# Hybrid layer with a 32-expert mixture: the second norm in halves, the router's steps reordered, the last adaLN product moved, the first projection and the final norm split

## The chip, the cores and the metric

The kernel runs on one core of one Trainium2 chip. The metric is the device time of one execution in microseconds (us); the numbers below come from one execution taken by the hardware profiler and from three timed runs.

## The reference, cut to what matters

One layer on 256 rows of 1024 (two tiles of 128 rows). `w_ada` gives six rows of 1024 (shift, scale and gate of both norms), in 12 column blocks of 512.

```python
mod = silu(c) @ w_ada + b_ada;  sh1, sc1, gt1, sh2, sc2, gt2 = split(mod, 6)
h = rms_norm(x, g_norm1) * (1 + sc1) + sh1
z = h @ w_in + b_in                      # 5376 columns: v, u, q, k, v, gate A, gate B
...                                      # gated MLP (A) and window attention (B)
x = x + gt1 * ((sigmoid(ga) * (ya @ w_o_a) + sigmoid(gb) * (yb @ w_o_b)) @ w_out)
h2 = rms_norm(x, g_norm2) * (1 + sc2) + sh2
top_v, top_e = top_k(h2 @ w_router + b_router, 4)      # of 32 experts; gates = softmax(top_v)
# expert e on its rows: gu = h2 @ w_gate_up[e] + b_gate_up[e]   (1024 x 2048, f32, 8 MiB)
#   hid = min(gu[:, :1024], 7) * sigmoid(1.702 * ...) * (clip(gu[:, 1024:], -7, 7) + 1)
#   y = hid @ w_down[e] + b_down[e]                             (1024 x 1024, f32, 4 MiB)
x = x + gt2 * sum(gate * y);  return rms_norm(x, g_final)
```

## The kernel before, in words

Five instruction streams are written out by hand and tied by semaphores (`ev(name)`): `sp` (SyncE) issues the large loads in a fixed order, `pe` multiplies, `dve` and `act` do the elementwise work, `pool` a few constants. Each engine runs its own stream strictly in the written order, so a wait holds everything behind it on that engine.

**Dense part.** Each projection is cut into items of 512 columns, in the order v0, v1, u0, u1, q0, q1, kv, ga0, ga1, gb0, gb1, oa0, oa1, ob0, ob1, out0, out1. An item's weights (2 MiB) go to one of three ring slots. VectorE splits them into an upper part (`w_parts_upper`, L810) and a remainder (`lower`, L367), as it does with the activations (`x_parts`, L834). TensorE then runs `rows_times` for each row tile: 24 matmuls (L1363), eight each of upper by upper, lower by upper and upper by lower. The adaLN blocks are spread between the items: `ada(j)` (L1385), a ScalarE copy (`part_copy`), `late_rows(j)` (L1396) and VectorE's `add_mod(j)`. `ada(11)` makes the second half of `gt2`; it stands between gb0 and gb1, and its weights sit in the room of slots 6 and 7.

**Slots.** An expert's weights are 12 pieces of 1 MiB: eight of gate_up, four of down. 22 slots (`store`) hold them, in rooms that the dense part frees bit by bit, so `sp` fills the slots for the first 22 pieces (`first_loads`, L392 and L410) one after another: 0, 1, 5, 10 and 11 when out1 is done, 18 when h2 is there, 16 after `logit_parts`, 21 after the logits, 20 when `start_acc` has put x into the accumulators (`acc_set`), 14 and 15 after the table of blocks. From then on `refill` loads a piece as soon as the piece 22 places earlier was used for the last time (`gu_used`, `down_used`, L398 and L410); it needs the order of the experts (`order_ready`).

**From the dense part to the experts.** VectorE subtracts the bfloat16 part of the expert biases (`bias_less`, L1105) while ScalarE makes that part (`bias_part`, L755). After out1 each row tile goes through `residual` (L1111, L1113), the product with `mul2` (L1128), ScalarE's sum of squares (L764) and square root (L767), a Newton step (`inverse_std`, L846 to L854) and the product that is h2 (L1130). Then come the transposes (L1374), router logits (L1630, L1637), top 4 (`mask`), ranks and counts (L1645 to L1651), block starts (L1664 to L1666), the map `sel` and `gather` of the first 32 rows (L1674), the table of each block's expert (`etab`, L1695), and `last_is_least` (L1228 to L1266), which exchanges expert 31 and the smallest expert so that the smallest is worked on last.

**Experts.** Each expert takes one block per 32 rows. A block on TensorE: gate_up (L1723), the accumulation of the block before (`combine`, L1687), the gather of the next (L1674), a transpose (L1743) and down (L1751). The loop is written for 11 experts a turn.

**End.** After the last accumulation ScalarE squares both row tiles (L793) and takes the root (L796), VectorE does the Newton step and four products with `g_final` (L1321), and `sp` stores the two tiles (L555).

## Time and profile before

| | us |
|---|---|
| median of three runs (lowest, highest) | 1267.49 (1265.68, 1269.41) |
| the profiled execution | 1268.17 |
| its span, first to last instruction | 1266.4 |
| dense part, start to the last matmul of out1 | 277.1 |
| from there to the first expert matmul | 31.5 |
| experts, first matmul to the last accumulation | 947.2 |
| from there to the end of the span | 10.5 |

Shares of the span that the engines are busy: TensorE 80%, VectorE 36%, ScalarE 13%, DMA 375 GB/s on average. Times in rows are us from the span's start. A share of the span is an average over stages with different limits, so each stage is read by itself.

### The profile page before, as it was taken

The page shows a single profiled execution, that of the slowest core. Times are in us where ns is not written, and L with a number is a line of the kernel's source. Part 1 is how long each engine was busy: PE and PEld are TensorE (multiplying, and loading weights), DVE is VectorE, ACT ScalarE, POOL GpSimd, SP SyncE. Part 2 cuts the span into 40 slices and gives each one's busy share as a digit, 9 for nine tenths or more (in the row PEclk, how much of TensorE's full clock was granted, in tenths as well). Part 3 has the DMA queues.
Part 4 walks back from the last instruction along what each step waited for, and adds up shares of the span by engine and source line. Part 5 has one row for each costly group of instructions (what it writes and reads, how often), then busy time and mean ns, then how long its engine had stood idle before and what let it go on. Part 6 is the DMA issues. An engine that isn't in the chain of part 4 may idle for free.

```text
span 1266.4 us, 25543 instructions
## 1 busy us (share of the span) xinstructions
PE 1012.1 (80%) x9961; PEld 476.1 (38%) x9962; DVE 454.1 (36%) x1101; ACT 164.4 (13%) x279; POOL 12.3 (1%) x39
## 2 busy tenths in 40 slices
PE   4799999977988668665899999899655589866874
PEld 1667777763433123111244334344211224311221
DVE  1885878875322112111133333233111113311222
ACT  2221223032111001000011111111000001100101
POOL 1100000000000000000000000000000000000000
PEclk9899999986999779777899999999887889987888
DMA  9987876797999999999969999939999997999996
GB/s 346 371 284 245 288 247 242 223 387 290 424 426 425 425 426 425 425 426 423 425 282 426 423 427 424 426 150 426 425 425 425 426 425 316 426 424 425 426 425 256
DMA packets 73034, 474.38 MB, mean 375 GB/s; under 512 B 7512, under 2 KB 9496, under 8 KB 39036
## 3 DMA queue, kind: packets, MB, share of 16 engines
q1 hardware_dynamic: 69888, 469.39, 90.5%
q10 hardware_dynamic: 2588, 3.03, 0.8%
q0 software_dynamic: 480, 0.83, 0.3%
q8 instruction: 59, 0.97, 0.3%
q14 instruction: 19, 0.16, 0.0%
HBM read 472.17 MB, written 1.06 MB: 374 GB/s over the span
## 4 chain that ended last, share of the span: by engine, by line
PE 41%; DMA 28%; SPq 24%; DVE 3%; issue 3%; ACT 1%; DVEq 0%; ACTq 0%
DMA gate_up<-in_w_down_dram 17%; SPq L410 13%; PE acc L1363 13%; PE bank L1723 12%; SPq L398 8%; PE bank L1751 7%; DMA down<-in_w_down_dram 5%; DMA gate_up<-in_w_gate_up_dram 3%; PE acc L1687 2%; PE bank L1674 2%; DMA gate_up<-in_w_in_dram 1%; SPq L387 1%; DMA gate_up<-in_w_ada_dram 1%; SPq L522 1%; PE bank L1385 1%
## 5 line engine op out<-in xcount | busy, mean ns | idle before, releaser
L1723 PE MATMUL bank<-gate_up,mod 128*32 128x512 f32 x2512 | 343.0, 680 | 115.5 <-DMA gate_up<-in_w_gate_up_dram 96.4
L1723 PEld LDWEIGHTS bank<-gate_up,mod 128*32 128x32 f32 x2512 | 82.2, 119 | 310.8 <-issue 176.9
L1751 PE MATMUL bank<-gate_up,mod 128*32 128x256 f32 x2528 | 150.8, 382 | 22.9 <-DMA gate_up<-in_w_down_dram 22.9
L1295 DVE TENSOR_SCALAR front<-bank 128x256 f32<-128x256 f32 x50 | 21.2, 425 | 346.9 <-PE bank L1723 346.9
L1363 PE MATMUL acc<-gate_up_r 128*128 128x512 f32 (+1 forms) x544 | 135.1, 395 | 7.6 <-DVE down_r L834 7.6
L789 ACT ACTIVATE front<-front 128x256 f32<-128x256 f32 x50 | 20.8, 417 | 854.5 <-DVE front L1295 854.5
L1363 PEld LDWEIGHTS acc<-gate_up_r 128*128 128x128 f32 x544 | 100.7, 192 | 33.8 <-DVE down_r L834 8.1
L1751 PEld LDWEIGHTS bank<-gate_up,mod 128*32 128x32 f32 x2528 | 75.4, 110 | 84.2 <-DMA gate_up<-in_w_down_dram 34.7
L1313 DVE TENSOR_TENSOR mod<-bank,mod 128x256 f32<-128x256 f32 x50 | 21.2, 425 | 204.3 <-PE bank L1751 204.3
L1723 PE MATMUL bank<-down,mod 128*32 128x512 f32 x448 | 61.4, 670 | 26.5 <-DMA down<-in_w_gate_up_dram 24.4
L1215 DVE TENSOR_SCALAR front<-front 128x2 f32 x100 | 22.9, 229 | 154.1 <-issue 152.6
L367 DVE TENSOR_TENSOR gate_up_r<-gate_up,gate_up_r 128x4096 fp32r<-128x4096 f32 (+1 forms) x17 | 73.1, 4299 | 0.5
L1363 PE MATMUL acc<-gate_up_r,down_r 128*128 128x512 f32 (+1 forms) x272 | 66.2, 386 | 0.0
L789 ACT ACT_TABLE_LOAD x50 | 64.2, 1283 | 7.3 <-DVE table L1221 6.5
L1687 PE MATMUL acc<-mod,front 32*128 32x256 f32 x816 | 62.0, 420 | 0.5 <-DVE mod L1313 0.5
L1687 PEld LDWEIGHTS acc<-mod,front 32*128 32x128 f32 x816 | 39.3, 198 | 52.7 <-issue 49.9
L1674 PE MATMUL bank<-h,front 128*32 128x256 f32 x816 | 55.7, 391 | 0.4 <-DVE front L1173 0.4
L1363 PEld LDWEIGHTS acc<-gate_up_r,down_r 128*128 128x128 f32 x272 | 50.8, 190 | 10.5
L1723 PE MATMUL bank<-x_room,mod 128*32 128x512 f32 x240 | 33.6, 671 | 16.8 <-DMA x_room<-in_w_gate_up_dram 16.8
L1751 PE MATMUL bank<-down,mod 128*32 128x256 f32 x512 | 32.5, 390 | 12.6 <-DMA down<-in_w_down_dram 12.6
L810 DVE CAST gate_up_r<-gate_up 128x4096 fp32r<-128x4096 f32 (+1 forms) x17 | 37.8, 2225 | 2.4 <-DMA gate_up<-in_w_in_dram 1.7
L1723 PEld LDWEIGHTS bank<-down,mod 128*32 128x32 f32 x448 | 14.6, 117 | 59.5 <-issue 34.4
(303 smaller groups left out, 670.1 us busy)
## 6 DMA issues: line engine op xcount, KB each, us to landing
gate_up<-in_w_gate_up_dram SPq DMA_DIRECT2D x87, 2048.0 KB, 38.1
gate_up<-in_w_down_dram SPq DMA_DIRECT2D x96, 1024.0 KB, 35.4
down<-in_w_gate_up_dram SPq DMA_DIRECT2D x21, 2048.0 KB, 36.0
gate_up<-in_w_ada_dram SPq DMA_DIRECT2D x12, 2048.0 KB, 13.9
x_room<-in_w_gate_up_dram SPq DMA_DIRECT2D x12, 2048.0 KB, 35.8
down<-in_w_down_dram SPq DMA_DIRECT2D x22, 1024.0 KB, 35.5
gate_up<-in_w_in_dram SPq DMA_DIRECT2D x10, 2048.0 KB, 9.7
gate_up<-in_w_gate_up_dram SPq DMA_DIRECT2D x12, 1024.0 KB, 8.2
```

What stands on the lines that cost most here:

```text
L367: return eng.tensor_tensor(w_lower[i % RING][:, chunks, 0:cols], ring[i % RING][:, chunks, 0:cols], w_upper[i % 2][:, chunks, 0:cols], ALU ...
L398: eng.dma_start(store_pair(at % SLOTS), w_gu_view[:, bass.ds(e, 1), k // 2, :, :].rearrange("p e a n -> p (e a) n"))\
L410: eng.dma_start(store(at % SLOTS), w_dn_view[:, bass.ds(e, 1), i, :].rearrange("p a n -> p (a n)"))\
L789: act.activation(g_sig, g_cap, ACT.Sigmoid, scale=ALPHA).then_inc(ev("sig_ready"), 1)
L810: return dve.tensor_copy(dst, src)
L1215: return dve.tensor_scalar(slots, slots_gates[:, bass.ds(e, 1), 0:2].rearrange("p a t -> p (a t)"), slot_base[:, bass.ds(g, 1)], None, ALU ...
L1295: dve.tensor_scalar(g_cap, banks[4][:, 0:HW], LIMIT, None, ALU.min).then_inc(ev("g_ready"), 1)
L1363: last = pe.matmul(bank[:, 0:cols], lhsT[:, k, rows], w[:, k, 0:cols], start=(n == 0 and k == 0), stop=(n == 2 and k == KC - 1))
L1674: last = pe.matmul(banks[6][q * BM:(q + 1) * BM, 0:HW], sel[:, t, :], in_runs(h2[:, t, :])[:, q], start=(t == 0), stop=(t == 1), skip_grou ...
L1687: last = pe.matmul(acc[:, q, t * HW:(t + 1) * HW], gT[rows, t * P:(t + 1) * P], y_sb[rows, :], start=False, stop=True, skip_group_check=True)
L1723: last = pe.matmul(banks[4][q * BM:(q + 1) * BM, :], xT[:, k * BM:(k + 1) * BM], w.rearrange("p a (i q n) -> p q a i n", q=NG, n=2 * BM)[: ...
L1751: last = pe.matmul(banks[7][q * BM:(q + 1) * BM, 0:HW], hidT[:, k * BM:(k + 1) * BM], in_groups(w[:, k % 2, :])[:, q], start=(k == 0), sto ...
```

## The change

The diff moves and splits steps; the arithmetic is the same but for the order of a few sums.

- **First projection.** v0's weights are loaded and split in two halves; VectorE takes the upper part of the first half before the modulation is ready, and makes one quarter of `hT` in ScalarE's place; TensorE starts v0 on row tile 0 when the first of these parts is there.
- **ada(11)** with its copy and `late_rows(11)` goes from the attention part to the transposes of h2; slots 6 and 7 are loaded after it instead of beside gb1.
- **Second norm by halves.** The sums of squares and products with `mul2` of columns 0 to 511 are done when out0 is there; `bias_less` stands between these steps; the Newton step has fewer operations; the square root's table is loaded early; h2 is made and transposed in halves.
- **Router.** The map and gather of the first rows come before the counts' sums are used; two `start_acc` come later; `last_is_least` is split in two, the first half before the block starts are read. Expert order: the smallest expert still goes last, but the experts behind its old place move up by one, where before expert 31 took that place.
- **Loads.** Slot 14 right after slots 10 and 11, then 6 and 7, 18, 16, 21, 20, and 15 when `etab` is there.
- **End.** Squares and products with `g_final` run on ScalarE and VectorE at once, on opposite halves of the accumulators; the square root's table is loaded before the last accumulation; each engine scales one row tile.

```diff
@@ banks @@
-z_order += [f"out{j}t{t}" for j in range(2) for t in range(TILES)]
-r_order = ["logit_parts", "logits", "rank", "starts", "etab"]
+z_order += [f"out{j}t{t}" for j in range(2) for t in range(TILES)] + ["part11", "am11"]
+r_order = ["logit_parts", "logits", "rank", "counts", "starts", "etab"]
...
@@ sync engine @@
-load(*dense[0][:2], "ada1")
+item_used(sp, "ada1")
+for a in range(2):
+    chunks = slice(4 * a, 4 * a + 4)
+    sp.dma_start(ring[0][:, chunks, :], dense[0][1].rearrange("(k p) n -> p k n", p=P)[:, chunks, :])\
+      .then_inc((v0_half_in, ring_in[0])[a], 16)
...
-    if names[i] == "gb1":
-        item_used(sp, "ada11")
-        first_load(sp, 6)
-        first_load(sp, 7)
...
-sp.wait_ge(ev("h2_ready"), TILES)
+sp.wait_ge(ev("bias_part_ready"), 4)
+first_loads((14,))
+item_used(sp, "ada11")
+first_loads((6, 7))
+sp.wait_ge(ev("h2_ready"), 2 * TILES)
 first_loads((18,))
 z_wait(sp, "logit_parts")
 first_loads((16,))
 z_wait(sp, "logits")
-first_loads(range(21, SLOTS))
+first_loads((21,))
 sp.wait_ge(ev("acc_set"), 1)
-first_loads(range(20, min(21, SLOTS)))
-sp.wait_ge(ev("table_ready"), 1)
-sp.wait_ge(ev("slots_ready"), 1)
-sp.wait_ge(ev("bias_part_ready"), 4)
-first_loads((14, 15))
+first_loads((20,))
+z_wait(sp, "etab")
+first_loads((15,))
...
@@ scalar engine @@
+def square(t, j, ready, into):
+    w = slice(j * COLS, (j + 1) * COLS)
+    act.wait_ge(ev(ready), t + 1)
+    act.activation(h2[:, t, w], x_sb[:, t, w], ACT.Square, accum_out=into).then_inc(ev("ssq_ready"), 1)
...
+act.activation(nt, var, ACT.Sqrt)
 act.wait_ge(ev("bias_rest_ready"), 1)
 bias_part(slice(QR, 2 * QR))
 bias_part(slice(2 * QR, P))
+act.wait_ge(ev("mul2_ready"), 1)
+for t in range(TILES):
+    square(t, 0, "x2_half", ssq[:, t:t + 1])
 act.wait_ge(ev("bias_rest_ready"), 2)
 bias_part(slice(2 * QR, P))
-row_norms("x2_ready", 3)
-copy_T(h2T, "h")
+for t in range(TILES):
+    square(t, 1, "x2_ready", mv[:, t, 0:1])
+    act.wait_ge(ev("var_ready"), 3 + t)
+    act.activation(rstd[:, t:t + 1], var[:, t:t + 1], ACT.Sqrt).then_inc(ev("std_ready"), 1)
...
+    if t == 0:
+        part_copy(11)
...
+act.activation(rstd, var, ACT.Sqrt)
+for b in range(2):
+    if b:
+        act.wait_ge(ev("scaled"), TILES)
+    for t in range(TILES):
+        act.activation(squares[:, b, t], acc[:, 2 * b:2 * b + 2, t * HW:(t + 1) * HW], ACT.Square,
+                       accum_out=(ssq, nt)[b][:, t:t + 1]).then_inc(ev("ssq_ready"), 1)
...
+act.activation(h2[:, 1, :], h2[:, 1, :], ACT.Copy, scale=rstd[:, 1:2]).then_inc(ev("out1_ready"), 1)
...
@@ vector engine @@
+dve.wait_ge(v0_half_in, 16)
+upper(w_upper[0][:, 0:4, :], ring[0][:, 0:4, :]).then_inc(ev("w_upper_half"), 1)
...
+bank = z_wait(dve, "xT01")
+for i in range(4):
+    k = 4 + i
+    last = dve.tensor_scalar(hT[:, k, 0:P], bank[:, i * P:(i + 1) * P], mul1[:, k:k + 1], mod_col[:, 0, k:k + 1],
+                             ALU.mult, ALU.add)
...
+upper(upper_a[:, :, first_tile], hT[:, :, first_tile]).then_inc(ev("hT_upper"), 1)
+dve.wait_ge(ring_in[0], 16)
+upper(w_upper[0][:, 4:8, :], ring[0][:, 4:8, :]).then_inc(ev("w_upper_ready"), 1)
...
+dve.tensor_tensor(hT_lower[:, :, first_tile], hT[:, :, first_tile], upper_a[:, :, first_tile], ALU.subtract)\
+   .then_inc(ev("hT_parts"), 1)
...
+lower(dve, 0, slice(0, 4)).then_inc(ev("w_lower_half"), 1)
+dve.wait_ge(ev("w_upper_ready"), 1)
+lower(dve, 0, slice(4, 8)).then_inc(ev("w_lower_dve"), 1)
...
+x_parts(hT, upper_a, hT_lower, "hT_parts", slice(P, 2 * P))
...
+    link(dve.tensor_scalar(first, inv, inv, half, ALU.mult, ALU.mult))
+    dve.scalar_tensor_tensor(inv, first, 1.5, inv, ALU.add, ALU.mult).then_inc(ev("rstd_ready"), 1)
...
-for t in range(TILES):
-    residual(0, t)
+residual(0, 0).then_inc(ev("x2_half"), 1)
+bias_less(slice(0, P), 1)
...
+for t in range(TILES):
+    scaled_by_mul2(t, 0)
 bias_less(slice(2 * QR, P), 3)
+dve.wait_ge(ev("ssq_ready"), 4)
...
+    link(scaled_by_mul2(t, 1))
+    norm_factor(t)
+    for j in range(2):
+        w = slice(j * COLS, (j + 1) * COLS)
+        dve.scalar_tensor_tensor(h2[:, t, w], merged[:, t, w], rstd[:, t:t + 1], sh2[:, w], ALU.mult, ALU.add)\
+           .then_inc(ev("h2_ready"), 1)
...
+add_mod(11)
...
+dve.tensor_tensor(y_sb, y_sb, gt2, ALU.mult).then_inc(ev("y_ready"), 1)
...
+bank = z_wait(dve, "rank")
...
+bank = z_wait(dve, "counts")
+blocks_of(nbT, bank[0:E, P:2 * P]).then_inc(ev("counts_ready"), 1)
+z_done(blocks_of(nbB, bank[:, 0:E]), "counts")
...
+dve.wait_ge(ev("xg_done"), 1)
+dve.transpose(xT, chunk_cols(banks[6][:, 0:HW])).then_inc(ev("xT_ready"), 1)
...
+def last_is_least():
+    dve.tensor_tensor(blocks_by_place[:, 0:E - 1], nb[:, 1:E], nb[:, 0:E - 1], ALU.subtract)
+    link(dve.scalar_tensor_tensor(key[row, :], nb, float(GMAX), experts, ALU.mult, ALU.add))
+    link(dve.memset(key[row, 0:2], 1.0e9))
+    link(dve.tensor_reduce(one[row, :], key[row, :], AX.X, ALU.min))
+    link(dve.tensor_scalar(least[row, :], key[row, :], one[row, :], None, ALU.is_equal))
+    link(dve.tensor_tensor(least_of, nb, least[row, :], ALU.mult))
+    link(dve.tensor_reduce(nb_a, least_of, AX.X, ALU.add))
+    link(dve.scalar_tensor_tensor(a, nb_a, -float(GMAX), one[row, :], ALU.mult, ALU.add))
+    link(dve.tensor_scalar(moved[row, :], experts, a, None, ALU.is_ge))
+    dve.scalar_tensor_tensor(starts_by_place, nb, nb_a, moved[row, :], ALU.subtract, ALU.mult)
+    link(dve.tensor_tensor(blocks_by_place[:, 0:E - 1], blocks_by_place[:, 0:E - 1], moved[row, 0:E - 1], ALU.mult))
+    dve.tensor_tensor(table[0:1, ORDER_AT:ORDER_AT + E - 1], experts[:, 0:E - 1], moved[row, 0:E - 1], ALU.add)
+    dve.tensor_copy(table[0:1, ORDER_AT + E - 1:ORDER_AT + E], a)
+    dve.tensor_copy(blocks_by_place[:, end], nb_a)
+    link(dve.tensor_tensor(blocks_by_place[:, 0:E - 1], blocks_by_place[:, 0:E - 1], nb[:, 0:E - 1], ALU.add))
+    dve.tensor_copy(table[0:1, GMAX + 1:GMAX + E], blocks_by_place[:, 1:E])
+last_is_least()
...
+def places_of_blocks():
+    blocks = iota_g[0:1, :]
+    dve.tensor_tensor(start_of, st, least[row, :], ALU.mult)
+    link(dve.tensor_tensor(starts_by_place, starts_by_place, st, ALU.add))
+    dve.tensor_reduce(one[row, :], start_of, AX.X, ALU.add)
+    dve.tensor_tensor(rest, en[:, end], nb_a, ALU.subtract)
+    dve.tensor_copy(table[0:1, GMAX + E + 1:GMAX + 2 * E], starts_by_place[:, 1:E])
+    link(dve.tensor_tensor(least_of, starts_by_place, blocks_by_place, ALU.add))
+    dve.tensor_tensor(back, one[row, :], en[:, end], ALU.subtract)
+    dve.tensor_scalar(table[0:1, GU_AT + 1:GU_AT + E], least_of[:, 1:E], float(KC), 1.0 - KC, ALU.mult, ALU.add)
+    dve.tensor_scalar(table[0:1, DOWN_AT + 1:DOWN_AT + E], least_of[:, 1:E], 4.0, -3.0, ALU.mult, ALU.add)
+    link(dve.tensor_scalar(steps_at[row, 0, :], blocks, one[row, :], nb_a, ALU.is_ge, ALU.mult))
+    dve.tensor_tensor(steps_at[row, 0, :], steps_at[row, 0, :], blocks, ALU.add)
+    link(dve.tensor_scalar(steps_at[row, 1, :], blocks, rest, back, ALU.is_ge, ALU.mult))
+    dve.tensor_tensor(table[0:1, BLOCK_AT:BLOCK_AT + GMAX], steps_at[row, 0, :], steps_at[row, 1, :], ALU.add)\
+       .then_inc(ev("order_ready"), 1)
+places_of_blocks()
...
+for b in (1, 0):
...
+    for t in range(TILES):
+        dve.tensor_tensor(in_groups(h2[:, t, :])[:, groups],
+                          acc[:, groups, t * HW:(t + 1) * HW].rearrange("p q (h n) -> p q h n", h=2),
+                          in_groups(g_final_row)[:, groups], ALU.mult).then_inc(ev("scaled"), 1)
...
+dve.tensor_scalar(h2[:, 0, :], h2[:, 0, :], rstd[:, 0:1], None, ALU.mult).then_inc(ev("out0_ready"), 1)
...
@@ tensor engine @@
-    pe.wait_ge(ev("w_upper_ready"), i + 1)
+    if name == "v0t0":
+        pe.wait_ge(ev("hT_upper"), 1)
+        pe.wait_ge(ev("w_upper_half"), 1)
...
-ada(11)
...
-late_rows(11)
...
-    pe.wait_ge(ev("h2_ready"), t + 1)
-    transposes(h2, "h", [t])
-for name in z_order[-NZ:]:
-    z_gone(pe, name)
-start_acc(0)
+    for h in range(2):
+        pe.wait_ge(ev("h2_ready"), 2 * t + h + 1)
...
+    if t == 0:
+        ada(11)
+late_rows(11)
...
-start_acc(1)
...
+start_acc(0)
+start_acc(1)
...
+pe.wait_ge(ev("sel_ready"), 1)
+gather()
...
+start_acc(2)
+start_acc(3).then_inc(ev("acc_set"), 1)
...
-z_gone(pe, "etab")
```

## Rows read from the trace of the kernel before

**Rows 1.** Page, part 2: GB/s moved in 40 equal slices of the span.

```profile
GB/s 346 371 284 245 288 247 242 223 387 290 424 426 425 425 426 425 425 426 423 425 282 426 423 427 424 426 150 426 425 425 425 426 425 316 426 424 425 426 425 256
```

**Rows 2.** Busy time in stretches (us A:B; each engine; then PEclk, DMA share, GB/s).

```profile
277.00:324.00 47.00, 31.08 (x255) 15.57 (x254) 28.48 (x120) 13.72 (x21) 1.37 (x7) 0.75 0.84 325
324.00:620.00 296.00, 220.69 (x2364) 78.01 (x2364) 63.83 (x209) 23.80 (x28) 0.00 (x0) 0.86 1.01 425
700.00:860.00 160.00, 149.75 (x1928) 62.60 (x1928) 52.26 (x170) 19.92 (x23) 0.00 (x0) 1.00 0.88 371
1100.00:1250.00 150.00, 104.33 (x1062) 36.01 (x1058) 29.75 (x97) 10.33 (x13) 0.00 (x0) 0.83 1.01 425
```

**Rows 3.** The chain of waits, its end: start, length, what ran.

```profile
1215.52 37.56 DMA gate_up<-in_w_down_dram
```

**Rows 4.** Timeline, TensorE: start, length, line, operation [idle before <-releaser].

```profile
275.14 1.98 PE L1363 MATMUL acc<-gate_up_r 128*128 128x512 f32 x8
...
308.65 1.93 PE L1723 MATMUL bank<-gate_up,mod 128*32 128x512 f32 x8 [3.36 <-issue]
```

**Rows 5.** Timeline of the first projection.

```profile
36.13 2.29 DVE L810 CAST gate_up_r<-gate_up 128x4096 fp32r<-128x4096 f32 x1 [1.71 <-DMA gate_up<-in_w_in_dram]
...
40.35 3.78 PE L1363 MATMUL acc<-gate_up_r 128*128 128x512 f32 x8 [6.41 <-DVE down_r L834]
...
45.26 1.22 DVE L834 TENSOR_TENSOR down_r<-down,gate_up_r 128x1024 fp32r<-128x1024 f32 x1
...
46.36 3.79 PE L1363 MATMUL acc<-gate_up_r 128*128 128x512 f32 x16
```

**Rows 6.** Busy time in a stretch after v1.

```profile
64.00:66.00 2.00, 2.00 (x19) 0.61 (x18) 1.30 (x3) 0.58 (x1) 0.00 (x0) 1.00 0.16 28
```

**Rows 7.** Timeline, TensorE: ada(11) and its rows.

```profile
185.53 1.92 PE L1385 MATMUL acc<-gate_up,x_room 128*32 128x512 f32 x16
...
194.06 0.43 PE L1396 MATMUL acc<-h,x_room 128*32 128x128 f32 x8
```

**Rows 8.** Timeline of the second norm, VectorE and ScalarE.

```profile
250.20 0.69 DVE L1087 TENSOR_TENSOR front<-acc,front 128x512 f32<-128x512 f32 x1 [2.26 <-PE acc L1363]
...
275.32 1.22 DVE L1105 TENSOR_TENSOR gate_up<-gate_up,mod 64x1024 f32<-64x1024 f32 x1 [4.10 <-ACT front L755]
...
277.71 0.69 DVE L1111 TENSOR_TENSOR down<-acc,front 128x512 f32<-128x512 f32 x1
...
288.70 1.28 DVE L1130 SCALAR_TENSOR_TENSOR h<-down,sm,front 128x1024 f32<-128x1024 f32 x1
```

**Rows 9.** Timeline of the router, with the first refill.

```profile
291.80 1.92 PE L1612 MATMUL acc<-x_room,ident 128*128 128x512 f32 x2
...
296.31 1.96 PE L1612 MATMUL acc<-x_room,ident 128*128 128x512 f32 x4
...
296.58 0.29 DVE L1137 TENSOR_TENSOR front<-bank,sm 128x32 f32<-128x32 f32 x2 [6.60 <-PE bank L1637]
...
314.63 0.97 SPq L410 DMA_DIRECT2D gate_up<-in_w_down_dram  x2
```

**Rows 10.** The DMA view: loads (queue, count, KB each, median us to landing).

```profile
gate_up<-in_w_down_dram SPq DMA_DIRECT2D x96, 1024.0 KB, 35.4
...
gate_up<-in_w_in_dram SPq DMA_DIRECT2D x1, 1024.0 KB, 5.0
```

**Rows 11.** Timeline of the end.

```profile
1255.95 1.02 ACT L793 ACTIVATE h<-acc 128x1024 f32<-128x1024 f32 x1 [8.18 <-PE acc L1687]
...
1258.09 1.28 ACT L796 ACT_TABLE_LOAD   x1
...
1260.61 2.73 DVE L1321 SCALAR_TENSOR_TENSOR h<-acc,sm,gate_up 128x512 f32<-128x512 f32 x4
...
1262.05 1.66 SPq L555 DMA_DIRECT2D out_dram<-h  x2
```

More of the change, by code:

```diff
@@ L105, in bass_hybrid_layer @@
     t_order += [f"m{t}{h}" for h in range(2) for t in range(TILES)]
[L106 removed]
+    t_order += [f"h{t}{h}" for t in range(TILES) for h in range(2)] + ["not_used", "gT"]
     ctx = ExitStack()
@@ L647, in _ @@
             for t in range(TILES):
-                for h in range(2):
+                for h in range(1 if t == 0 else 2):
                     name = f"xT{t}{h}"
@@ L1168, in _ @@
-            blocks_of(nbT, bank[0:E, 2 * P:3 * P]).then_inc(ev("counts_ready"), 1)
-            link(blocks_of(nbB, bank[:, 2 * E:3 * E]))
-            def gather_map(g, slots):
-                for t in range(TILES):
-                    last = dve.tensor_scalar(sel[:, t, :], iota_q[:, 0, :], slots[:, t:t + 1], None, ALU.is_equal)
-                return last
-            z_done(dve.tensor_scalar(dtmp.rearrange("p t e -> p (t e)"), bank[:, 0:TILES * E], 1.0, None, ALU.add), "rank")
-            z_gone(dve, "rank")
@@ new lines, in _ @@
+            nb_a, a, rest, back = (few[row, i:i + 1] for i in range(4))
+            least_of, start_of, starts_by_place, blocks_by_place = (lasts[row, i, :] for i in range(4))
+            def last_is_least():
[15 more added lines that the diff above has]
+                dve.tensor_copy(table[0:1, GMAX + 1:GMAX + E], blocks_by_place[:, 1:E])
@@ L1692, in _ @@
             gather()
+            pe.wait_ge(ev("counts_ready"), 1)
+            pe.wait_ge(ev("counters"), 5)
+            bank = z_open("starts")
+            pe.matmul(bank[:, 0:E], nbT, tri_exc[:, 0:E], start=True, stop=True, skip_group_check=True)
+            pe.matmul(bank[:, 2 * E:2 * E + 2], tri_exc, nbT[:, 0:2], start=True, stop=True, skip_group_check=True)
+            last = pe.matmul(bank[:, 2 * E + 2:2 * E + 4], tri_inc, nbT[:, 0:2], start=True, stop=True,
+                             skip_group_check=True)
+            z_put(last, "starts")
+            pe.wait_ge(ev("gates_ready"), 1)
+            bank = t_open("gT")
+            for t in range(TILES):
+                last = pe.transpose(bank[:, t * P:(t + 1) * P], selg[:, t, :], ident[:, :])
+            t_put(last, "gT")
+            start_acc(2)
+            start_acc(3).then_inc(ev("acc_set"), 1)
             pe.wait_ge(ev("cmp_ready"), 1)
```

265 lines of the change are left out of this document (125 added, 140 removed).

## Prediction, made before the changed kernel was run

> **What bounds the kernel now.** I read the slices first. From the eleventh slice on the core moves 423 to 427 GB/s, except in the slices at 282, 150, 316 and the last [rows 1]. The stage table says what the exceptions are: where 425 GB/s flow, TensorE is busy for only 221 of 296 us and 104 of 150 us, and where 371 flow it is busy for 150 of 160 us [rows 2]. So the expert loop waits for weights, and in three places, where experts with three to five blocks follow each other, the weights wait for TensorE. The chain of waits ends in a load of down weights, 37.56 us from issue to landing [rows 3]: the end is set by the last piece of one stream.
>
> So I ask when this stream starts. The dense part ends at 275.14 + 1.98 = 277.1, and the first expert matmul runs at 308.65 [rows 4]. From 277 to 324 us the DMA moved 325 GB/s x 47 us = 15.3 MB, or 14.6 pieces of 1.0486 MB [rows 2]. Eleven of them are first loads that the code issues after out1 (slots 0, 1, 5, 10, 11, 18, 16, 21, 20, 14, 15), so 3.6 pieces of refill had landed by 324. One piece takes 1.0486 MB / 425.5 GB/s = 2.464 us (between the 425 and 426 of most slices, [rows 1]). The refill stream therefore runs as if it had begun at 324 - 3.6 x 2.464 = **315.2**. From there to the end the order of waits repeats, and I take the end to move as this start moves.
>
> **The change part by part.**
>
> *First projection.* TensorE starts v0 at 40.35; ahead of it VectorE casts all of the weights (2.29 us), waiting 1.71 us for them, and makes both parts of hT [rows 5]. After the change the cast no longer stands ahead of the first matmul (one half is done earlier, the other follows), nor does the remainder (1.22): 2.29 + 1.22 = 3.5 us less, and I add back 0.4 because the first half cast now stands before the modulation column. That is a start near 37.2. Row tile 1 began at 46.36 + 8 x 0.237 = 48.3 and cannot begin before hT's second parts, done at 45.26 + 1.22 = 46.5 [rows 5]; these come some 0.6 us earlier, as half of the cast left the chain. The lead is 48.3 - 45.9 = 2.4 at most, 1.8 if they do not move; I take **2.2**. If both halves of the weights land together at 36.13, the modulation column waits for them and the lead becomes about -0.5: that is the other bound. Later the loads of q0 and ada(5) are issued as v1 ends, and the DMA was idle there (28 GB/s, [rows 6]), so the lead passes.
>
> *ada(11)* leaves TensorE's full stretch: 1.85 + 0.35 = **2.2** us net of overlap [rows 7]. VectorE had been waiting 2.26 us for TensorE at the end of ob1 [rows 8], so it does not become the bound. If it did, 0 would be left. The dense part thus ends 4.4 earlier, at 272.7 (bounds 276.6 and 272.4).
>
> *Second norm.* Before, residual(1, 0) began at 277.71 although its product was there, since `bias_less` had waited 4.10 us for ScalarE; ScalarE then loaded the root's table (1.28, as in [rows 11]); h2 was done at 288.70 + 1.28 = 290.0, 12.9 after the dense part [rows 8]. After, tile 0 is through when out1 ends, and tile 1 needs: the rest of tile 0's h2 0.8, two residual steps 1.4, the product 0.7, square, root and short Newton step 1.3, h2's halves 1.3, together 5.5 (each 512 columns at 0.69, [rows 8]). That is 7.4 less. `ada(11)` falls into TensorE's wait between the tiles; its rows cost at most 2 at the end.
>
> *Router.* The logits' sum stood 296.58 - 277.1 = 19.5 after the dense part, the first matmul 12.1 later [rows 4, 9]. Now one `start_acc` (1.0 to 1.9, [rows 9]) has left the way to the logits: 9.6 to 12 after. The gather comes earlier, but TensorE still issues `etab` ahead of the experts, and that waits for `cmp_ready`, which now has the first half of `last_is_least` ahead of it on VectorE: 16 steps at half of the pair's 0.29, 2.3 us. About 1.3 us of block sums and table entries leave this place. So 12.1 + 2.3 - 1.3 = 13 from the sum to the first matmul; two `start_acc` now stand before the ranks, two more before `etab`, and where each takes 1.9 instead of 1.0 the way grows by 3.6, to 16.6. The first refill stood 314.63 - 296.58 = 18.1 after the sum [rows 9]; `order_ready` needs 29 small steps instead of 32, half of them done while TensorE works, so 16 to 18.5 now. The first refill can be issued at 272.7 + 9.6 + 16 = 298.3, at the latest near 303.
>
> *First loads.* These now queue without a gap: 0, 1, 5, 10, 11 at 272.7, 14 right behind, 6 and 7 when ada(11) has run (near 276 to 279), 18, 16, 21, 20, 15 each asked for before those ahead have landed. `sp`'s new wait for ada(11) holds 6, 7 and all behind them, but it ends while the six loads ahead of it run on to 288. It is two pieces more than before: the move of ada(11) takes 4.9 us of stream out of an idle place and puts it here. 13 x 2.464 = 32.0, plus 0.9 for the start (a load with little ahead takes 5.0 to land, 2.5 of it moving, [rows 10]; between 0 and 2.5). The stream of refills begins at 272.7 + 0.9 + 32.0 = **305.6**, after 298.3: so what is late next is the DMA, and the router's gain is cover, not path. Gain 315.2 - 305.6 = **9.6**. The Trainium skill, page "DMA: Bandwidth & Descriptors", section Specifications, gives a core about 358 GB/s from HBM; this kernel's 425 [rows 2] contradicts that.
>
> *Order of the experts.* Counts worked out from the reference's inputs give 50 blocks; the smallest is expert 3, so the two-block expert 31 moves from fourth place to the last but one, and the others come one place sooner. A block is 64 + 8 + 16 + 16 + 2 + 64 = 170 matmuls, so 700 to 860 holds 1928 / 170 = 11.3 blocks of 149.75 / 11.3 = 13.2 us [rows 2]. Two take less than a load of 12 x 2.464 = 29.6, and the runs of large experts keep their neighbours, so I take **0**; bounds -1 and +1.
>
> *End.* From 1255.95 to the span's end at 1266.4 it took 10.5: two squares, the table 1.28, root and Newton step, four products 2.73, store [rows 11]. After: four 512-column products on VectorE beside four squares on ScalarE, 2.8; sums, root and Newton step 1.6; one scaling 1.1 (a 1024-column activation takes 1.02, [rows 11]); the last store as before 3.1. That is 8.6, a gain of **1.8** (1.0 to 2.3). The table load that vanishes ends at 1259.37, and 1.24 later the products begin, with the root and five Newton steps between [rows 11]. The Trainium skill, page "ScalarE: Activation LUTs", section What ACT_TABLE_LOAD costs, adds about 1.4 of drain to each switch; by it the gain would be 3.2, but 1.24 us hold no such drain.
>
> **Sum.** 9.6 + 1.8 = 11.4. The profiled execution took 1268.17 (span 1266.4 and 1.8 around it), so 1256.8; the median of the runs shown is 0.7 lower: **1256.1**.
>
> **The rivals.**
> *The front's lead is lost* (halves landing together, or TensorE waiting at ada(5) all the same). Against it: the idle DMA [rows 6]. The dense part ends 1.7 to 2.2 earlier: 1258.3 to 1258.8. Chance 0.15.
> *The router bounds the refill*, or the new order does not do what it says: if the first refill stays 314.63 - 277.1 = 37.5 after the dense part, it is at 310.2, and the gain is about 4.4 + 1.8: 1261.3. For it: the work put ahead of `cmp_ready`; against it: h2 stands 7.4 us nearer to the dense part's end. 0.08.
> *A slow first stream.* The slice at 253 to 285 moved 387 GB/s [rows 1]; at that rate 13 pieces take 35.2, 3.2 more: 1259.3. 0.04. By the Trainium skill's 358 (the page above) it would be 38.1, so 1262.2.
> *A larger lead in the dense part*, as ScalarE's exponentials no longer wait behind the copy of ada(11): 6 instead of 4.4, so 1254.5, or 1253 with a better end. 0.07.
> *Slower:* the last two pieces reuse the slots of expert 31's first two, which are now free only in its second block. If the queue has run dry by then, one block (13.2) and a lone load's extra 2.5 [rows 10] are added: 1271.8. It decides when the lead of a load in the loop, 35.4 from issue to landing [rows 10], falls under 13; it does not look so. 0.03.
>
> **How the numbers follow.** The forecast holds 0.63, with its own range 1254.5 to 1257.7. To 1252.5 and 1261.5 the range takes in the larger lead, the lost front and the slow router, and leaves out the worst. What a measurement can tell from no change is about 0.3%, 3.8 us: faster 0.93, within it 0.04 (a router and a front that both fail), slower 0.03.
>
> **What would show it.** Right: out1's last matmul near 272.7, the first expert matmul between 295 and 299, the first refill issued before 303, the DMA at 425 GB/s without a gap from there into the loop, the three PE-bound stretches about 9.6 earlier with the same length, some 8.6 us from the last accumulation to the end. Wrong: a gap in the DMA between the first loads and the refills (router), out1 ending after 274 (front), a stretch under 420 GB/s behind the last large expert (order), or a span that shrinks by more than the start moved. The weakest term is the dense part's lead, as it alone moves everything behind it.

## The result and the profile after

The changed kernel takes **1260.64 us** (1257.45 to 1262.39); the kernel before, on the same chip, 1267.49 (1264.61 to 1269.41). The ratio is 0.9942, with an interval from 0.9926 to 0.9958. The change is faster by 6.85 us; 11.4 were forecast. The time lies inside the range, near its upper end, and about 4.5 us of the gain did not come. They are the subject of what follows.

The page's row of GB/s by slice (40 slices of 31.5 us) has the dips of [rows 1], but the one in the tenth slice (290 GB/s, 285 to 317 us) has gone, and a small one, 405, is new (the 24th, 725 to 756 us):

```profile
GB/s 343 376 287 245 277 250 197 225 409 423 425 424 426 425 426 425 425 424 426 274 424 425 425 405 423 134 426 427 425 425 426 425 314 425 425 425 427 425 425 269
```

The first projection, the dense part's end and the first expert matmul, from the timeline of TensorE after (start us, duration us, engine, line, what, times, and in brackets the idle time before it and what ended that); they answer to [rows 4, 5]:

```profile
37.49 3.75 PE L1455 MATMUL acc<-gate_up_r 128*128 128x512 f32 x8 [3.15 <-DVE gate_up_r L837]
...
45.98 2.10 PE L1455 MATMUL acc<-gate_up_r 128*128 128x512 f32 x8 [0.66 <-DVE down_r L861]
...
78.66 3.37 PE L1477 MATMUL bank<-gate_up,x_room 128*32 128x512 f32 x16 [2.49 <-DMA gate_up<-in_w_ada_dram]
...
271.42 1.98 PE L1455 MATMUL acc<-gate_up_r 128*128 128x512 f32 x8
...
295.76 1.06 PE L1822 MATMUL bank<-gate_up,mod 128*32 128x512 f32 x8 [1.93 <-issue]
```

The dense part ends at 273.4 (277.1 before), and the first expert matmul comes 12.9 us earlier. Next, three stretches of the kernel after, from the view of stretches (its last two columns are the busy share of the DMA engines and GB/s, the one before them TensorE's granted clock): the issue of ada(5)'s load, ada(5) itself, and the first loads with what follows.

```profile
64.00:66.00 2.00, 2.00 (x12) 1.36 (x8) 1.97 (x5) 1.48 (x2) 0.00 (x0) 1.00 0.86 306
...
78.60:82.20 3.60, 3.54 (x17) 0.83 (x18) 3.53 (x4) 1.20 (x3) 0.00 (x0) 0.55 1.05 404
...
272.00:324.00 52.00, 42.63 (x455) 19.76 (x453) 28.50 (x129) 11.68 (x21) 1.37 (x7) 1.00 1.01 418
```

From 272 to 324 us the transfers run on at 418 GB/s, which at 425 leaves 0.9 us idle; before, 277 to 324 moved 325 GB/s [rows 2]. The first refill, from the timeline of SP's queue after (314.63 before, [rows 9]):

```profile
299.24 1.90 SPq L415 DMA_DIRECT2D gate_up<-in_w_down_dram  x2
```

**Where the time went** can be read at two products that wait for a landing: the last product of place 9 (the tenth expert in order, 120 pieces into the weights in every kernel here), and the last of the loop. Timeline of TensorE, first the kernel before, then the kernel after:

```profile
561.06 1.07 PE L1751 MATMUL bank<-gate_up,mod 128*32 128x256 f32 x16 [1.41 <-DMA gate_up<-in_w_down_dram]
...
1253.12 1.07 PE L1751 MATMUL bank<-gate_up,mod 128*32 128x256 f32 x16 [1.11 <-DMA gate_up<-in_w_down_dram]
```

```profile
552.45 1.07 PE L1850 MATMUL bank<-gate_up,mod 128*32 128x256 f32 x16 [1.19 <-DMA gate_up<-in_w_down_dram]
...
1247.77 1.07 PE L1850 MATMUL bank<-gate_up,mod 128*32 128x256 f32 x16 [0.39 <-DMA gate_up<-in_w_down_dram]
```

Place 9 ends 8.6 us earlier: the start of the stream came forward nearly as forecast. The last product is only 5.35 us earlier: 3.26 us are lost inside the loop, behind place 9. The rest of the span, 13.28 us before and 12.33 after from the start of that last product, gives 0.95. Together -8.61 + 3.26 - 0.95 = -6.3, the difference of the two spans (1266.4 and 1260.1).

Of the places where this could be lost one stands out in the chain of waits of the kernel after (start us, length us, what the chain waited in):

```profile
625.54 7.34 issue
632.88 1.93 PE bank L1822 x8
634.81 1.94 issue
637.37 8.47 PE bank L1822 x47
```

For 7.34 us TensorE issues nothing although it waits for nothing that the profile shows. It is the only stall of this kind above 2 us in the loop. Here TensorE's loop over experts, unrolled by eleven (`TURN`), jumps back, between places 10 and 11. The kernel before has it too, and waits for a load again 13 us later:

```profile
599.01 1.94 PE L1723 MATMUL bank<-gate_up,mod 128*32 128x512 f32 x8 [7.36 <-issue]
...
611.68 1.92 PE L1723 MATMUL bank<-gate_up,mod 128*32 128x512 f32 x16 [1.47 <-DMA gate_up<-in_w_gate_up_dram]
```

What differs is the neighbour. Before, expert 11 with its four blocks stood at place 11, behind the jump, in a stretch where TensorE waits for weights anyhow. The new order moves it to place 10, ahead of the jump: the stall now ends a run of four blocks in which the weights wait for TensorE. The view of waits of the kernel after, TensorE, 585 to 858 us (in total, times, longest), has no load in it; the next wait for one ends at 858.31:

```profile
PE bank L1822 <- issue: 12.3, 8, 7.3
PE bank L1829 <- issue: 1.9, 1, 1.9
```

### The profile page after: what moved, and what is told of

Read it like the earlier page. It is cut to its first block, busy times and chain, and to the rows that moved or that the text cites. A ratio compares the mean times of both kernels' runs of the same rounds, so it can differ in the third digit from the quotient of the medians.

```text
span 1260.1 us, 25572 instructions
## 1 busy us (share of the span) xinstructions
PE 1011.7 (80%) x9961; PEld 472.6 (38%) x9962; DVE 457.2 (36%) x1109; ACT 165.5 (13%) x286; POOL 12.2 (1%) x39
## 3 DMA queue, kind: packets, MB, share of 16 engines
HBM read 472.17 MB, written 1.06 MB: 376 GB/s over the span
## 4 chain that ended last, share of the span: by engine, by line
PE 43%; SPq 25%; DMA 22%; DVE 4%; issue 4%; ACT 1%; DVEq 0%; ACTq 0%
SPq L403 15%; PE bank L1822 15%; PE acc L1455 11%; DMA gate_up<-in_w_down_dram 10%; PE bank L1850 8%; SPq L415 7%; DMA down<-in_w_down_dram 6%; DMA gate_up<-in_w_ada_dram 3%; DMA x_room<-in_w_down_dram 3%; PE acc L1770 2%; PE bank L1757 2%; SPq L392 1%; SPq L529 1%; PE bank L1477 1%; PE bank L1842 1%
## 5 line engine op out<-in xcount | busy, mean ns | idle before, releaser
L1822 PE MATMUL bank<-gate_up,mod 128*32 128x512 f32 x2128 | 300.6, 693 | 125.2 <-DMA gate_up<-in_w_gate_up_dram 108.7
L1822 PEld LDWEIGHTS bank<-gate_up,mod 128*32 128x32 f32 x2128 | 68.9, 120 | 297.2 <-issue 150.4
L1850 PE MATMUL bank<-gate_up,mod 128*32 128x256 f32 x2272 | 135.8, 383 | 23.9 <-DMA gate_up<-in_w_down_dram 23.0
L1822 PE MATMUL bank<-down,mod 128*32 128x512 f32 x768 | 99.7, 645 | 24.6 <-DMA down<-in_w_gate_up_dram 22.7
L1850 PEld LDWEIGHTS bank<-gate_up,mod 128*32 128x32 f32 x2272 | 68.4, 110 | 79.2 <-DMA gate_up<-in_w_down_dram 33.0
L1822 PEld LDWEIGHTS bank<-down,mod 128*32 128x32 f32 x768 | 25.2, 116 | 79.4 <-issue 50.3
L1822 PE MATMUL bank<-x_room,mod 128*32 128x512 f32 x304 | 43.5, 687 | 13.7 <-DMA x_room<-in_w_gate_up_dram 13.3
L1850 PE MATMUL bank<-down,mod 128*32 128x256 f32 x544 | 35.1, 397 | 7.9 <-DMA down<-in_w_down_dram 7.9
(317 smaller groups left out, 692.4 us busy)
## 6 DMA issues: line engine op xcount, KB each, us to landing
gate_up<-in_w_ada_dram SPq DMA_DIRECT2D x12, 2048.0 KB, 14.1
down<-in_w_down_dram SPq DMA_DIRECT2D x22, 1024.0 KB, 35.8
```

What stands on the lines that cost most here:

```text
L1822: last = pe.matmul(banks[4][q * BM:(q + 1) * BM, :], xT[:, k * BM:(k + 1) * BM], w.rearrange("p a (i q n) -> p q a i n", q=NG, n=2 * BM)[: ...
L1850: last = pe.matmul(banks[7][q * BM:(q + 1) * BM, 0:HW], hidT[:, k * BM:(k + 1) * BM], in_groups(w[:, k % 2, :])[:, q], start=(k == 0), sto ...
```

## The experiments

All ratios are to the kernel before, measured beside each kernel; in brackets their 95% intervals.

**Order: another expert goes last.**

```diff
-                link(dve.memset(key[row, 0:2], 1.0e9))
+                link(dve.memset(key[row, 0:18], 1.0e9))
```

> The changed kernel with one number altered: the least expert is sought among 18 to 31, so that expert 18 goes last and experts 0 to 17 keep their own places; expert 11 (four blocks) is at place 11 again, behind the turn of TensorE's expert loop and not ahead of it. Theory A (the 7.34 + 1.94 us in which TensorE issues nothing at the loop's turn cost time only where TensorE is the later of the two): the stall falls ahead of expert 11, where TensorE waits for weights, as in the kernel before; the transfers' idle time behind the large experts goes back from 42.8 to some 39 us and the time is 1257 us (1255.8 to 1258.3). Theory B (the order has no price, the lost 4 to 5 us are at the front of the loop or at its end): 1260.6 us, within 1 us, and the idle time stays near 42.8.

Measured: 1254.45 us, ratio 0.9900 (0.9884 to 0.9915). One number in the table of the order is worth 0.4% (0.9942 to 0.9900); the time is 1.3 us under Theory A's range, and its three stretches of idle transfers hold 37.0 us, not 39. The stall is still there, ahead of expert 11 now:

```profile
589.00 1.93 PE L1822 MATMUL bank<-gate_up,mod 128*32 128x512 f32 x8 [7.94 <-issue]
```

**Jump: 22 experts to a turn.** With 32 experts that is one turn and ten experts behind it, so nothing jumps back. SyncE's loop over the refills uses `TURN` too, and its jump goes with it.

```diff
-TURN = 11
+TURN = 22
```

> The changed kernel, order of the experts and all, with the loop over experts unrolled by 22 and not by 11 (one turn of 22 and 10 behind it), on all engines that use it: no jump back is left between places 10 and 11. Theory A: no issue stall of 7 us behind the four-block expert; the stretch from 583 to 837 us on TensorE gets 3 to 9 us shorter, and the time is 1257 us (1255.8 to 1258.3). Theory B (the order or the loop's turn has no price): 1260.6 us within 1 us. A third outcome, a stall of the same size at another place among one-block experts, would say that it hangs on the amount of code and not on the jump; the time is then 1257 us too, since a TensorE that waits for weights covers it.

Measured: 1255.01 us, ratio 0.9906 (0.9893 to 0.9919). The order is that of the changed kernel, and the stall has gone: at 621.74, where place 11 begins, 0.40 us are left of it. The time is 0.8 us under Theory A's range. What the stream lost shows in the view of stretches (last column GB/s), first the kernel after, then this one:

```profile
600.00:620.00 20.00, 20.00 (x250) 8.03 (x246) 6.39 (x23) 1.70 (x2) 0.00 (x0) 1.00 0.49 188
730.00:740.00 10.00, 10.00 (x136) 4.08 (x128) 2.11 (x8) 0.00 (x0) 0.00 (x0) 1.00 0.88 349
790.00:820.00 30.00, 30.00 (x381) 12.27 (x377) 10.58 (x36) 3.40 (x4) 0.00 (x0) 1.00 0.30 120
1020.00:1040.00 20.00, 20.00 (x256) 8.30 (x252) 8.81 (x29) 3.40 (x4) 0.00 (x0) 1.00 0.62 248
```

```profile
600.00:620.00 20.00, 20.00 (x272) 8.79 (x264) 7.55 (x24) 3.40 (x4) 0.00 (x0) 1.00 0.66 267
730.00:740.00 10.00, 9.61 (x126) 4.33 (x130) 2.61 (x10) 0.10 (x1) 0.00 (x0) 1.00 1.03 431
780.00:810.00 30.00, 30.00 (x388) 12.47 (x384) 9.93 (x33) 3.40 (x4) 0.00 (x0) 1.00 0.35 140
1010.00:1030.00 20.00, 20.00 (x246) 7.94 (x242) 7.12 (x25) 2.37 (x4) 0.00 (x0) 1.00 0.60 250
```

At 425 GB/s a stretch of t us that moves r GB/s lacks t x (1 - r/425): 11.2 + 1.8 + 21.5 + 8.3 = 42.8 us of idle transfers after, 7.4 + 0 + 20.1 + 8.2 = 35.8 here. Two things make the 7 us. Behind expert 11, TensorE is late by the stall of 7.34 + 1.94, and 1.8 + 1.4 us reach the stream at 730 and 790 us. And in the stretch at 600, 3.7 us are lost *ahead* of the jump. There the last down piece of expert 11's first block lands late; kernel after, then 22 to a turn:

```profile
579.50 1.07 PE L1850 MATMUL bank<-x_room,mod 128*32 128x256 f32 x16 [1.22 <-DMA x_room<-in_w_down_dram]
583.41 1.26 PE L1850 MATMUL bank<-x_room,mod 128*32 128x256 f32 x16 [2.85 <-DMA x_room<-in_w_down_dram]
584.44 1.94 PE L1822 MATMUL bank<-gate_up,mod 128*32 128x512 f32 x8
```

```profile
578.43 1.07 PE L1850 MATMUL bank<-x_room,mod 128*32 128x256 f32 x16 [1.23 <-DMA x_room<-in_w_down_dram]
580.91 1.07 PE L1850 MATMUL bank<-x_room,mod 128*32 128x256 f32 x16 [1.41 <-DMA x_room<-in_w_down_dram]
581.80 1.04 PE L1822 MATMUL bank<-gate_up,mod 128*32 128x512 f32 x8
```

The gap between the last two products is 3.91 us and not 2.48. After the longer wait the granted clock is 0.79 from 584 to 592 us (1.00 with 22 to a turn, 582 to 590), so the next eight matmuls take 1.94 and not 1.04.

The edit does one thing more. In all nine profiles with 11 to a turn TensorE pauses for 0.68 to 0.78 us where it goes from one expert to the next inside the loop without a wait for weights; in the five with 22 to a turn these pauses are 0.35 to 0.55. Behind expert 11 there are seven up to 850 us, together 4.97 us in the kernel after and 2.80 here, so 2.2 us of what TensorE gains here are not the jump's. No run separates the two. The order's edit leaves these pauses as they are and wins as much.

**Both at once.** The edits of the two kernels above together.

> The changed kernel with expert 18 last and with 22 experts to a turn, both at once; it completes the square of order and jump. Expert 18 last alone gave 1254.45 us, 22 to a turn alone 1255.01, the kernel before 3.4 us less for 22 to a turn in either order. Theory A (a stall ahead of the large expert is free, one behind it costs 5 to 6 us): nothing is left to gain, 1254.5 us (1253.5 to 1255.5). Theory C (the jump back costs some 3 us wherever it falls, and in the changed kernel the new order costs something beside it): 1251.3 us (1250.3 to 1252.5).

Measured: 1256.29 us, ratio 0.9903 (0.9885 to 0.9921). This is Theory A's "nothing left", though 0.8 us above its range: the two edits are two ways to the same gain, so in the changed kernel order and jump cost time only together.

**The changed kernel again.**

> The changed kernel once more, as it is. Two questions: does it come out near 1260.6 us again (1259 to 1261.5), and does the last down piece of expert 11's first block land late again (2.85 us of wait, and 3.9 us between the last two products, where the kernels with 22 to a turn show 1.41 and 2.48)? If it does, the late piece belongs to the price of order and jump together; if not, it is chance of one execution, and the stall behind the four-block expert is what is left.

Measured: 1260.18 us, ratio 0.9934 (0.9918 to 0.9951). The price is there again, and so is the late piece (2.93 us of wait, 3.97 between the products). This time the granted clock behind it is 1.00 (583 to 591 us) and the next eight matmuls take 1.06, so the price stands without the slow matmuls.

**The same edits on the kernel before.** First the new order alone (the shifting table of the change in place of the old swap, at its old place), then `TURN = 22` alone, then both.

> The kernel before with the new order of the experts alone (least expert taken out, all behind it one place earlier; the same table built at the old place in the program). Theory A: the loop's turn falls behind the four-block expert, TensorE's stretch there takes 9 us longer, of which 3 to 4 reach the transfers: 1271 us (1269.5 to 1272.5), 0.2 to 0.4% slower than the kernel before. Theory B (the order has no price): 1267.5 us, within 0.1%.

Measured: 1267.40 us, ratio 0.9997 (0.9988 to 1.0007). Theory A's number was wrong here. The stall stands behind expert 11 as it says (7.02 us), but expert 11 at place 10 leaves less idle time in its own stretch, 7.6 us instead of 10.5. That the two cancel is not shown, as the next two runs tell. There is no late piece here (2.47 us between the two products).

> The kernel before with nothing altered but the unrolling, 22 experts to a turn and not 11. Theory A (the stall at the loop's jump back costs only where TensorE is late): in the kernel before the 7.36 us stand at 599 us, where TensorE waits for weights with or without them; the stall goes, the time does not move: 1267.9 us, within 1 us. Theory B (a longer turn is worth 5 to 6 us for itself, whatever the order): 1262 us.

Measured: 1264.68 us, ratio 0.9969 (0.9957 to 0.9981). Theory A had 0 here; 3.4 us came, and by the ratio 3.9. The profiled execution of this kernel, at 1268.21, was the slowest of its runs and shows no gain, so the trace doesn't tell where it lies.

> The kernel before with the new order of the experts and 22 experts to a turn. With the new order alone the transfers idle for 39.4 us in the loop (38.9 with the old order), of which the stretches at 730 and 790 us hold 3.1 us that the kernels without a stall behind expert 11 do not have; the stretch at 610 us is 2.9 us shorter than with the old order. Theory A (the new order gains 2.9 us, the stall behind it takes 3.1 back): 1264.4 us (1263.2 to 1265.6). Theory B (order and stall have no price in the kernel before): 1267.5 us.

Measured: 1264.52 us, ratio 0.9968 (0.9955 to 0.9980), the number of Theory A, but not its reason: the old order reaches the same without the 2.9 us that Theory A gives to the new one. The stretch at 730 us is back to 419 GB/s (345 with the order alone). So 22 to a turn gains 0.3% in the kernel before in either order, 0.3 to 0.4% in the changed kernel in the new order (0.9942 and 0.9934 against 0.9906) and nothing that can be measured with expert 18 last (0.9900 against 0.9903). What order and jump do together shows in the changed kernel alone. Why the edit gains in the old order of the kernel before stays open. The shorter pauses are a candidate: eight from 660 to 880 us are 5.68 us before and 3.32 with 22 to a turn.

**The front's lead.** First ada(5) behind u1 tile 0:

```diff
                 rows_times(item, 0, h_parts)
+                if n == 3:
+                    ada(5)
                 pe.wait_ge(ev("hT_parts"), 2)
...
-                if n:
+                if n in (1, 3):
                     ada(n + 3)
```

> The changed kernel with the product ada(5) moved on TensorE from ahead of u1 tile 0 to behind it. In the changed kernel ada(5) waits for its weights until 78.66 us and takes 3.37 us, so that u1 tile 0 starts at 82.02 us as in the kernel before (82.09), and the front's lead of 2.3 us is gone. Theory A (the lead ends at ada(5) and nowhere else, and the dense part's end sets the start of the refill stream): u1 tile 0 starts near 76.2 us, the dense part ends 3 to 4.2 us earlier, and the time is 1257 us (1256.2 to 1258). Theory B (another load sets the pace right behind it, so that the lead ends at a later product): the dense part ends as it does now, 1260.6 us within 1 us.

Measured: 1260.49 us, ratio 0.9934 (0.9921 to 0.9947): no gain. u1 tile 0 starts near 77.2 instead of 82.0, but ada(6), whose load is asked for when ada(5) is done, then waits for weights until 93.68; the dense part ends at 271.7, 1.7 earlier (0.3 earlier than in the second profile of the changed kernel, 272.0), and order and jump are still there. Then the front undone, in the kernel with 22 to a turn:

```diff
-                sp.dma_start(ring[0][:, chunks, :], dense[0][1]...[:, chunks, :])\
-                  .then_inc((v0_half_in, ring_in[0])[a], 16)
+            load(*dense[0][:2], "ada1")
...
+            w_parts_upper(0)
+            for t in range(TILES):
...
+                x_parts(hT, upper_a, hT_lower, "hT_parts", slice(t * P, (t + 1) * P))
```

> The changed kernel with 22 experts to a turn and with the first projection's new order (weights of v0 in two halves, cast by halves, second transposed quarter on VectorE) undone. Prediction's reading (the front's lead of 2.2 us passes to the start of the stream): 1257.2 us (1256.3 to 1258.2), dense part's end about 2 us later than 272.4. Rival (the lead ends at ada(5)): 1255.0 us, within 0.8.

Measured: 1256.82 us, ratio 0.9913 (0.9893 to 0.9933) beside 0.9906: not to be told apart. TensorE starts v0 at 40.32 instead of 39.29, u1 tile 0 at 82.05 instead of 81.12, and the dense part ends at 273.3 instead of 272.4.

**The router's cover.** VectorE steps without use behind `z_wait(dve, "logits")`, 24 and then 64 of them, in the kernel with expert 18 last:

```diff
             bank = z_wait(dve, "logits")
+            for _ in range(24):
+                link(dve.memset(few[0:1, 4:8], 0.0))
```

> The changed kernel with expert 18 last, and 24 linked VectorE steps without use (5 to 7 us by the 0.2 to 0.29 us of such steps) put between the router's logits and its first sum. Prediction's reading (the router's end is cover, since the queue of first loads holds the stream): the first refill is issued at 305 to 307 instead of 299.96 us, the first loads run until about then, and the time is 1254.5 to 1256.5 us. Rival (the router's end sets the start of the refills): 1259.5 to 1261.

Measured: 1254.73 us, ratio 0.9894 (0.9877 to 0.9912). The delay was weaker than meant: the first refill moved by 0.87, to 300.83, so this run tells little of the cover.

> The changed kernel with expert 18 last and 64 VectorE steps without use ahead of the router's first sum. With 24 of them the steps took 2.4 to 2.8 us, of which a wait for TensorE took up 1.84, and the first refill moved from 299.96 to 300.83 us only. 64 take 7.4 us, 5.5 net: the first refill is issued near 305.5. With two first loads fewer a refill issued at 304.46 left a gap of 3.2 us in the transfers; with all 13 the queue lasts 4.9 us longer. Prediction's reading (cover): 1254.5 to 1256.5 us, with a gap of at most 2 us. Rival (the router's end sets the start): 1259 to 1260.5.

Measured: 1258.65 us, ratio 0.9919 (0.9903 to 0.9935), by the ratios 2.4 us above the 0.9900 without steps. That lies between the two forecasts, as the delay was stronger than meant: the first refill came at 308.00 and not 305.5, and the transfers now have a gap; stretch from 295 to 315 us, with 64 steps and without:

```profile
295.00:315.00 20.00, 18.95 (x150) 8.44 (x152) 13.58 (x79) 3.37 (x4) 0.00 (x0) 0.79 0.79 310
```

```profile
295.00:315.00 20.00, 17.71 (x202) 6.84 (x206) 8.28 (x39) 2.98 (x3) 0.00 (x0) 0.91 1.02 424
```

The gap is 20 x (1 - 310/425) = 5.4 us, so a refill asked for by about 308.0 - 5.4 = 302.6 is free. This is 30.8 us after the dense part's end in this profile (271.8). The first refill stands 28.5 after it with expert 18 last and 25.8 in the changed kernel: the router's end is cover by 2.3 and 5 us.

**ada(11) back at its old place**, in the kernel with expert 18 last; with it the loads 6 and 7:

```diff
             rows_times("gb0", 1, h_parts)
+            ada(11)
             attend(1)
             rows_times("gb1", 0, h_parts)
+            late_rows(11)
...
+                if names[i] == "gb1":
+                    item_used(sp, "ada11")
+                    first_load(sp, 6)
+                    first_load(sp, 7)
```

> The changed kernel with expert 18 last, and ada(11), its copy, its rows and the first loads 6 and 7 back at their old places. By the prediction's sum the dense part ends 2.2 us later, and 11 first loads stand behind it and not 13, which is 4.9 us less: 2.7 us faster than with expert 18 last alone, 1251.8 us (1250.5 to 1253). Rival (with the stream free earlier, the router's end is what the refills wait for): 1253 to 1255, and a gap in the transfers ahead of the first refill. If the dense part's end does not count: 1249.5.

Measured: 1257.04 us, ratio 0.9921 (0.9898 to 0.9944), so no gain. The rival's gap is there, though the time lies 2.0 us above its range: the first refill is asked for at 304.46, and the stretch from 295 to 315 moves 376 GB/s, a gap of 20 x (1 - 376/425) = 2.3 us. Against the 4.9 us of stream that are taken out here stand this gap and a dense part that ends 3.2 us later (274.7 against 271.5), together 5.5; place 9 ends at 551.0, with expert 18 last alone at 550.5.

## Why the prediction came out as it did

Order "own" in this table is that with expert 18 last. Time from the last product of place 9 to the loop's last product, worked out from the two landings as shown above (in brackets place 9's own time):

| kernel | order, turn | us |
|---|---|---|
| before | old, 11 | 692.1 (561.1) |
| after | new, 11 | 695.3 (552.5) |
| after, again | new, 11 | 693.0 (551.0) |
| ada(5) late | new, 11 | 696.5 (550.6) |
| expert 18 last | own, 11 | 690.2 (550.5) |
| 22 to a turn | new, 22 | 688.0 (551.4) |
| both | own, 22 | 689.7 (552.6) |
| front undone | new, 22 | 689.6 (552.1) |

The others, in the same way: expert 18 last with 24 steps 688.4, with 64 steps 691.8, with ada(11) back 690.2; the kernel before with the new order 691.7, with 22 to a turn 692.4, with both 689.9.

- *First projection.* Right at its place: v0 starts at 37.49 (37.2 forecast), row tile 1 2.3 us earlier (2.2). In the other profiles with the new front v0 starts at 37.1 to 39.3. "So the lead passes" failed in the profiled execution. The idle DMA of [rows 6] was used (306 GB/s), but ada(5)'s load took 14.1 us and not 13.6, and behind the wait of 2.49 the clock was granted at 0.55, mostly its lower level of 1.2 GHz (1.00 before, after a wait of 1.93): 3.37 us and not 1.92. u1 tile 0 begins at 82.0 as before. In other executions part of the lead stays (81.12, and 80.24 with expert 18 last), and in the second profile of the changed kernel all of it: ada(5) at 77.31 behind a wait of 1.48, u1 tile 0 at 79.17. Yet undoing the front moved no time that can be measured.
- *ada(11)* gave its 2.2 (the product chain at 216.34 before starts at 214.12). The dense part ends at 273.4, forecast 272.7; the other profiles with this front and ada(11) at its new place give 271.5 to 273.7. The outer bound of 276.6 does not follow from its terms (a lead of -0.5 and 0 for ada(11) make 277.6), but nothing hangs on it.
- *Second norm and router.* The logits' sum comes at 284.05, 10.6 after the dense part (9.6 to 12 forecast, though the terms give 19.5 - 7.4 - 1.9 = 10.2 for the 9.6), the first matmul 11.7 later (13 to 16.6), the first refill 15.2 later (16 to 18.5). That the stream, not the router, sets the start holds, with 5 us to spare by the run with 64 steps; a cover of 7 was forecast.
- *First loads.* Right: 0.9 us idle, as in the sum, and place 9 ends 8.5 to 10.6 us earlier than before in the seven profiles of the table, for 9.6 forecast.
- *Order of the experts* is the step that failed. "The runs of large experts keep their neighbours, so I take 0; bounds -1 and +1" looked at the weights of the neighbours only. Against the same kernel with either half of the cause taken away, the order together with the jump costs 0.28 to 0.42% by the ratios, 3.5 to 5.3 us, and in the table 5.5 us (694.9 on average against 689.4). In the profile of the kernel after about half of it, 3.7 of 7 us of idle transfers, lies at the late piece, whose cause stays open. The kernel before does not show this price: 691.7 with the new order and the jump, 692.1 with the old. The stall was in the trace of before, at 599 us, ahead of a stretch in which TensorE waits for weights again, and the prediction did not ask what would stand around it after the shift.
- Its companion "the three PE-bound stretches with the same length" fell with it: 42.8 us of idle transfers after, 40 in its second profile, against 39 before.
- *End.* 1.0 and not 1.8. Engines' steps came as forecast. From the timeline after:

```profile
1250.60 0.60 ACT L817 ACTIVATE gate_up<-acc 128x512 f32<-128x512 f32 x1 [5.95 <-PE acc L1770]
...
1254.92 0.75 DVE L1402 TENSOR_SCALAR h<-h,sm 128x1024 f32<-128x1024 f32 x1
1254.98 1.15 ACT L823 ACTIVATE h<-h,sm 128x1024 f32<-128x1024 f32 x1 [1.08 <-DVE sm L881]
1255.70 0.83 SPq L562 DMA_DIRECT2D out_dram<-h  x2
```

  The failed term is "the last store as before 3.1": from the last product's end to the span's end it is now 4.0. What stays the same is the time from the *first* store's issue, 4.35 before (1262.05 to 1266.4) and 4.40 after (1255.70 to 1260.1). Before, the first tile's store ran while the second tile was computed; now both tiles are done within half a microsecond, and both stores lie behind them.

Of the rivals, the lost front came true in part, as told; the one on the slower side did not: the last product waits 0.39 us for its landing, and no gap opens ahead of it. The slow router and the slow first stream did not come (the first refill at 299.24 and not 310.2, the first loads at 418 GB/s and not 387), nor did a larger lead.

So of the 11.4 forecast 6.3 came between the two spans: 1.0 too much for the start, 0.8 for the end, and 3.3 us for a loop that got longer. In the second profile of the changed kernel, the fastest run of its six, the loop is 1.0 longer than before. With order or jump taken out the sum would have stood well: 1254.45 and 1255.01 for the two single edits, 1256.1 forecast. In part that is luck, since the loop then is also 2 to 4 us shorter than before (table), which nobody forecast.

**What lies behind the stall.** The runs show 6.9 to 7.9 us without issue where the loop jumps back and none where it does not jump. They also show an instruction queue (q8) at work in it. First the kernel after, 625.5 to 635 us, then the kernel before, 591.6 to 601:

```profile
q8 instruction: 2, 0.03, 1.3%
q14 instruction: 2, 0.02, 0.4%
```

```profile
q8 instruction: 2, 0.03, 1.4%
```

All nine profiles with the jump have two packets of q8 in the stall and the eight matmuls behind it; elsewhere in the loop of the kernel after there are two to five in 80 us. Queue q14 does not belong to it: in the kernel before its three nearest packets come at 616 to 628 us, long after the stall. With 22 to a turn no packet of either lies between 613 and 622 us, where place 11 begins. The Trainium skill, page "Runtime: NRT & Kernel Launch", section Instruction fetch mechanics, has the rule: "A taken branch whose target isn't in the current 2-page window forces a DMA fetch of the target page before execution can continue". The trace agrees in where the stall and the packets are. Why it takes 7 us no run shows.

## What to carry to other kernels

Before you reorder work in an unrolled loop, find in the old trace every stall that costs nothing where it is, the jump back of the loop above all, and ask what stands in front of it afterwards. In the changed kernel the jump back cost 0.3 to 0.4% behind the longest run of work and nothing that can be measured ahead of a wait; in the kernel before its place made no difference, so try it in the kernel that you have. In a kernel bound by one stream, follow two landings, an early and the last one, through all versions; their difference separates what the start gained from what the loop lost. Two stores that become ready together are not one store's time.
